# Mamba-2 scan of a decoder trunk without a chunk state, and with a group's sum of squares moved into the next group's insertion

## The reference, cut to what matters

```python
def step(state, inp):                    # L = 128, two chunks
    cum = jnp.cumsum(dtc * a, axis=1)
    decay = jnp.exp(jnp.where(causal, cum[:, :, None] - cum[:, None], -jnp.inf))
    w = jnp.einsum('bign,bjgn->bijg', cc, bc)[..., None] * decay * dtc[:, None]
    y = jnp.einsum('bijgh,bjghp->bighp', w, xc)
    y = y + jnp.einsum('bign,bghpn->bighp', cc, state) * jnp.exp(cum)[..., None]
    wts = jnp.exp(last[:, None] - cum) * dtc
    state = state * ... + jnp.einsum('bjgh,bjghp,bjgn->bghpn', wts, xc, bc)
# then: y + d_skip*x, times silu(z), RMS norm over each group's 512 channels, norm weight, w_out
```

## Time and profile before

| | us |
|---|---|
| median of 3 runs | 2580.13 (2579.45 to 2582.21) |
| the profiled execution | 2579.37 |
| its span | 2577.7 |
| PE busy | 2571.5 (100% of the span), granted clock full in all 40 slices |
| DVE busy | 1791.5 (70%) |
| ACT busy | 1419.8 (55%) |
| POOL busy | 220.4 (9%) |
| chain of work that ended last | PE 95%, DVE 3%, ACT 1% |

### The profile page before, as it was taken

How to read it: one execution, slowest core, us unless ns; L and a number is a source line. 1 busy time by engine, 2 the same in 40 slices (tenths; PEclk the granted TensorE clock), 3 DMA queues, 4 the chain that set the end, 5 groups by cost and what they waited for, 6 DMA issues and landing times.

```text
span 2577.7 us, 46139 instructions
## 1 busy us (share of the span) xinstructions
PE 2571.5 (100%) x15247; PEld 2255.1 (87%) x15247; DVE 1791.5 (70%) x2592; ACT 1419.8 (55%) x2190; POOL 220.4 (9%) x197
## 2 busy tenths in 40 slices
PE   9999999999999999999999999999999999999999
PEld 8888888888888888888888888888888888888888
DVE  8777777775677777776555686777777777775454
ACT  6776766754455555554444465665555555554333
POOL 0211122212100000000111000102200000000000
PEclk9999999999999999999999999999999999999999
DMA  6655555556555555556666576324555555556665
GB/s 213 234 193 192 195 196 195 196 179 188 188 188 190 189 186 191 190 191 183 191 190 190 193 235 198 121 98 137 183 191 189 187 189 191 190 187 187 189 190 169
DMA packets 139483, 481.59 MB, mean 187 GB/s; under 512 B 17329, under 2 KB 19441, under 8 KB 138384
## 3 DMA queue, kind: packets, MB, share of 16 engines
q1 hardware_dynamic: 136448, 467.20, 56.7%
q0 software_dynamic: 2368, 12.68, 1.4%
q10 hardware_dynamic: 592, 0.71, 0.1%
HBM read 478.28 MB, written 2.16 MB: 186 GB/s over the span
## 4 chain that ended last, share of the span: by engine, by line
PE 95%; DVE 3%; ACT 1%; issue 0%; DMA 0%; ACTq 0%; DVEq 0%
PE ps L844 49%; PE ps L843 26%; PE pq L844 6%; PE po L844 4%; PE pq L843 3%; PE po L843 2%; DVE w_lo L1268 1%; PE po L1151 1%; PE pq L1137 0%; PE ps L975 0%; PE ps L977 0%; PE ps L976 0%; PE ps L958 0%; PE pq L861 0%; PE po L965 0%
## 5 line engine op out<-in xcount | busy, mean ns | idle before, releaser
L1268 DVE TENSOR_TENSOR w_lo<-raw,w_hi 128x1024 fp32r<-128x1024 f32 (+1 forms) x896 | 1094.5, 1224 | 617.7 <-ACT w_hi L441 616.5
L441 ACT ACTIVATE w_hi<-raw 128x1024 fp32r<-128x1024 f32 (+1 forms) x896 | 933.5, 1043 | 808.1 <-PE ps L844 702.9
L844 PE MATMUL ps<-xn,w_hi 128*128 128x512 f32 x3904 | 1359.2, 392 | 0.0
L843 PE MATMUL ps<-xn,w_lo 128*128 128x256 f32 x3904 | 1098.3, 281 | 0.3 <-DVE gpad L1277 0.2
L844 PEld LDWEIGHTS ps<-xn,w_hi 128*128 128x128 f32 x3904 | 730.5, 187 | 159.6
L843 PEld LDWEIGHTS ps<-xn,w_lo 128*128 128x128 f32 x3904 | 737.8, 189 | 4.1 <-issue 1.5
L844 PE MATMUL ps<-hid,w_hi 128*128 128x512 f32 x1408 | 488.2, 391 | 0.0
L843 PE MATMUL ps<-hid,w_lo 128*128 128x256 f32 x1408 | 394.2, 280 | 0.0
L844 PEld LDWEIGHTS ps<-hid,w_hi 128*128 128x128 f32 x1408 | 263.3, 187 | 57.7
L843 PEld LDWEIGHTS ps<-hid,w_lo 128*128 128x128 f32 x1408 | 266.1, 189 | 0.0
L844 PE MATMUL pq<-xn,w_hi 128*128 128x512 f32 x528 | 185.3, 393 | 0.0
(11 more groups left out here) (300 smaller groups left out, 2461.4 us busy)
## 6 DMA issues: line engine op xcount, KB each, us to landing
raw<-w_gu SPq DMA_DIRECT2D x352, 512.0 KB, 3.9
raw<-w_ssm_in SPq DMA_DIRECT2D x158, 512.0 KB, 3.8
raw<-w_down SPq DMA_DIRECT2D x128, 448.0 KB, 3.4
raw<-w_nsa_in SPq DMA_DIRECT2D x82, 512.0 KB, 4.4
raw<-w_ssm_out SPq DMA_DIRECT2D x64, 512.0 KB, 4.4
raw<-w_down SPq DMA_DIRECT2D x64, 512.0 KB, 3.6
raw<-w_nsa_out SPq DMA_DIRECT2D x32, 512.0 KB, 4.4
wcum<-cum_scratch POOLq DMA_DIRECT2D x8, 1024.0 KB, 7.7
```

The lines of the kernel that those rows point to most:

```text
L441: act.activation(w_hi[:, slot, 0:n * P], raw[:, slot, 0:n * P], ACT.Copy).then_inc(unit_rounded, 1)
L843: pe.matmul(acc[:, n:2 * n], w_lo[:, slot, cols], x[:, kb, 0:n], start=(kb == 0), stop=False, skip_group_check=True)
L844: mm = pe.matmul(acc[:, 0:2 * n], w_hi[:, slot, cols], x[:, kb, 0:2 * n], start=False, stop=(kb == n_blocks - 1), skip_group_check=True)
L1268: TT(w_lo[:, slot, 0:n * P], raw[:, slot, 0:n * P], w_hi[:, slot, 0:n * P].bitcast(F32), ALU.subtract).then_inc(unit_split, 1)
```

## The change

The scan loses its state. `scan_turn` now has one product of B of the first chunk with C of both chunks (128x256) and one of B and C of the second chunk (128x128); the transpose of B, the state product and ACT's copy of the state are gone, `xw` stays as DVE made it, and POOL multiplies `cex` with the B0·C1 product from `sbt` (one third of it) where it took C from `bc`. `scan_y` is the same otherwise.

A group's sum of squares moves from behind unit 14 of its own scan pass to behind unit 0 of the next pass, ahead of the next group's `scan_turn`, and into another bank (`ps[7]`). What depends on it moves too: the root from step 14 to step 3 of the next pass, the scaling from 15 to 4, the rounding from 16 to 6, the rest from 17 to 7. The tables have a second number, 1 or 2, for how many groups back. POOL's skip term goes into a buffer of its own, `skip`, which lies where `y_ssm` lies; POOL no longer waits there for the previous group's `y_ready`.

```diff
@@ ACT
-            def scan_state(g):
-                act.wait_ge(state_done, g + 1)
-                act.activation(xw[:], ps[4][:], ACT.Copy).then_inc(state_ready, 1)
@@
-            SCAN_ACT = ((1, scan_sbt), (3, scan_ecum), (3, lambda g: scan_decay(g, 0)), (4, lambda g: scan_decay(g, 1)),
-                        (6, scan_state), (11, scan_square), (14, scan_std), (16, scan_round))
+            SCAN_ACT = ((1, 1, scan_sbt), (3, 2, scan_std), (3, 1, scan_ecum), (3, 1, lambda g: scan_decay(g, 0)),
+                        (4, 1, lambda g: scan_decay(g, 1)), (6, 2, scan_round), (11, 1, scan_square))
@@ ACT, last_scan_step
+                for at, back, stage in ((1, 1, scan_sbt), (2, 2, scan_std), (2, 1, scan_ecum), (2, 1, lambda g: scan_decay(g, 0)),
+                                        (2, 1, lambda g: scan_decay(g, 1)), (2, 1, lambda g: scan_decay(g, 2)), (4, 2, scan_round),
+                                        (6, 1, scan_square), (8, 1, scan_std), (9, 1, scan_round)):
@@ PE
-                pe.wait_ge(gstd_ready, g)
                 pe.wait_ge(yz_step, 2 * g)
...
-                    pe.matmul(ps[4][:, cut], bc[:, 0, cut], bc[:, 1, cut], start=True, stop=True)
-                pe.transpose(ps[4][:, 2 * L:3 * L], bc[:, 0, 0:L], ident[:]).then_inc(turned, 1)
-
-            def scan_state(g):
-                pe.wait_ge(xw_ready, g + 1)
-                pe.wait_ge(sbt_ready, g + 1)
-                pe.matmul(ps[4][:], sbt[:, 2 * L:3 * L], xw[:], start=True, stop=True).then_inc(state_done, 1)
+                pe.matmul(ps[4][:, 0:2 * L], bc[:, 0, 0:L], bc[:, 1], start=True, stop=True)
+                pe.matmul(ps[4][:, 2 * L:3 * L], bc[:, 0, L:T], bc[:, 1, L:T], start=True, stop=True).then_inc(turned, 1)
@@
             def scan_sumsq(g):
+                total = ps[4] if is_body(g, GROUPS - 1) else ps[7]
                 pe.wait_ge(sq_summed, g + 1)
-                pe.matmul(ps[4][:, 0:T], ones[:], xdt[:, 0, 0:T], start=True, stop=True).then_inc(gss_done, 1)
+                if not is_body(g, GROUPS - 1):
+                    pe.wait_ge(tile_out, ph["ssm"].tile0 + 9 + (g + 1) * ph["ssm"].per_body)
+                pe.matmul(total[:, 0:T], ones[:], xdt[:, 0, 0:T], start=True, stop=True).then_inc(gss_done, 1)
@@
-            SCAN_PE = ((0, scan_turn), (4, scan_state), (9, scan_y), (14, scan_sumsq))
+            SCAN_PE = ((0, 2, scan_sumsq), (0, 1, scan_turn), (9, 1, scan_y))
@@ PE, first body of ssm_out
-                for at, stage in ((0, scan_turn), (3, scan_state), (6, scan_y), (8, scan_sumsq)):
+                for at, back, stage in ((0, 2, scan_sumsq), (0, 1, scan_turn), (6, 1, scan_y), (8, 1, scan_sumsq)):
@@ DVE
-                    pair = yz[:, 2 * b:2 * b + 2].rearrange("p a t -> p (a t)")
-                    last = TT(pair, ps[2 + b][:], pair, ALU.add)
+                    last = TT(yz[:, 2 * b:2 * b + 2], ps[2 + b][:].rearrange("p (a t) -> p a t", a=2),
+                              skip[:, bass.ds(g * XT_G + 2 * b, 2), 0:T], ALU.add)
@@
-            SCAN_DVE = ((1, scan_xdt), (5, scan_w), (10, scan_yz), (15, scan_norm), (17, scan_rest))
+            SCAN_DVE = ((1, 1, scan_xdt), (4, 2, scan_norm), (5, 1, scan_w), (7, 2, scan_rest), (10, 1, scan_yz))
@@ DVE, last_scan_step
-                for at, stage in ((1, scan_xdt), (6, scan_yz), (8, scan_norm), (9, scan_rest)):
+                for at, back, stage in ((1, 1, scan_xdt), (2, 2, scan_norm), (5, 2, scan_rest), (6, 1, scan_yz), (8, 1, scan_norm),
+                                        (9, 1, scan_rest)):
@@ POOL
                 pool.wait_ge(conv_act, g * 6 + 6)
-                pool.wait_ge(y_ready, g)
...
-                pool.tensor_tensor(yz[:], xf[:], cst[:, bass.ds(g * XT_G + CONST["ssm_d"], XT_G)].unsqueeze(2).broadcast_to([P, XT_G, T]),
+                pool.tensor_tensor(skip[:, bass.ds(g * XT_G, XT_G), 0:T], xf[:], cst[:, bass.ds(g * XT_G + CONST["ssm_d"], XT_G)].unsqueeze(2).broadcast_to([P, XT_G, T]),
                                    ALU.mult).then_inc(xd_ready, 1)
...
-                pool.tensor_tensor(cex[:], cex[:], bc[:, 1, L:T].unsqueeze(1).broadcast_to([P, GH, L]), ALU.mult).then_inc(cex_ready, 1)
+                pool.wait_ge(sbt_ready, g + 1)
+                pool.tensor_tensor(cex[:], cex[:], sbt[:, L:2 * L].unsqueeze(1).broadcast_to([P, GH, L]), ALU.mult).then_inc(cex_ready, 1)
```

More of the change, by code:

```diff
@@ L201, in trunk @@
                 dt_odd = sb("dt_odd", [HEADS, T], F32, st2)
+            with ExitStack() as st3:
+                skip = sb("skip", [P, S_TILES, 2 * T], F32, st3)
             y_ssm = sb("y_ssm", [P, S_TILES, 2 * T], F32R, st)
@@ L513, in conv_silu @@
                     act.wait_ge(xd_ready, g)
-                else:
-                    act.wait_ge(cex_ready, g)
                 act.wait_ge(turned, g)
@@ L549, in scan_std @@
             def scan_std(g):
+                total = ps[4] if is_body(g, GROUPS - 1) else ps[7]
                 act.wait_ge(gss_done, g + 1)
-                act.activation(grs[:], ps[4][:, 0:T], ACT.Sqrt, scale=1.0 / (XT_G * P), bias=eps[:, 0:1]).then_inc(gstd_ready, 1)
+                act.activation(grs[:], total[:, 0:T], ACT.Sqrt, scale=1.0 / (XT_G * P), bias=eps[:, 0:1]).then_inc(gstd_ready, 1)
             def scan_round(g):
@@ L573, in ssm_body @@
                     if scan:
-                        for at, stage in SCAN_ACT:
-                            if at == v:
-                                stage(g - 1)
+                        for at, back, stage in SCAN_ACT:
+                            if at == v and (back == 1 or not is_body(g, 1)):
+                                stage(g - back)
                     else:
@@ L980, in scan_sumsq @@
             def scan_sumsq(g):
+                total = ps[4] if is_body(g, GROUPS - 1) else ps[7]
                 pe.wait_ge(sq_summed, g + 1)
-                pe.matmul(ps[4][:, 0:T], ones[:], xdt[:, 0, 0:T], start=True, stop=True).then_inc(gss_done, 1)
+                if not is_body(g, GROUPS - 1):
+                    pe.wait_ge(tile_out, ph["ssm"].tile0 + 9 + (g + 1) * ph["ssm"].per_body)
+                pe.matmul(total[:, 0:T], ones[:], xdt[:, 0, 0:T], start=True, stop=True).then_inc(gss_done, 1)
             p = ph["ssm"]
-            SCAN_PE = ((0, scan_turn), (4, scan_state), (9, scan_y), (14, scan_sumsq))
+            SCAN_PE = ((0, 2, scan_sumsq), (0, 1, scan_turn), (9, 1, scan_y))
             def ssm_body(g, scan=True):
                 for v in range(0 if scan else 4, p.body):
+                    if scan and v == 6 and not is_body(g, 1):
+                        pe.wait_ge(gstd_ready, g - 1)
                     gemm_unit(p, g, v, xn)
                     if scan:
-                        for at, stage in SCAN_PE:
-                            if at == v:
-                                stage(g - 1)
+                        for at, back, stage in SCAN_PE:
+                            if at == v and (back == 1 or not is_body(g, 1)):
+                                stage(g - back)
                     elif v == 15:
@@ L1395, in scan_w @@
                 for c in range(2):
-                    last = TT(wcum[:, :, c], wcum[:, :, c], sbt[:, c * L:(c + 1) * L].unsqueeze(1).broadcast_to([P, GH, L]), ALU.mult)
+                    last = TT(wcum[:, :, c], wcum[:, :, c], sbt[:, 2 * c * L:(2 * c + 1) * L].unsqueeze(1).broadcast_to([P, GH, L]), ALU.mult)
                 last.then_inc(w_ready, 1)
@@ L1436, in ssm_body @@
                     if scan:
-                        for at, stage in SCAN_DVE:
-                            if at == v:
-                                stage(g - 1)
+                        for at, back, stage in SCAN_DVE:
+                            if at == v and (back == 1 or not is_body(g, 1)):
+                                stage(g - back)
                     if taps:
```

19 lines of the change are left out of this document (10 added, 9 removed).

## The result

The changed kernel takes 2599.25 us (median of 4, 2599.09 to 2599.79) against 2579.92 us (median of 4, 2579.45 to 2582.21): 19.3 us more, a ratio of 1.0074 with a 95% interval of 1.0061 to 1.0086. It is slower, as forecast, inside the range of 2584 to 2602, and 5.2 us above the predicted 2594.1. Its profiled execution took 2599.3 us with a span of 2597.6, which is 19.9 above the span of before.

The account below looks back on a forecast made before the run. PE's work bounds the kernel as long as every unit is split before PE comes to it. Terms -6.2 - 1.7 + 16.8 + 3.2 + 1.8 = +13.9 us on 2579.4, plus 0.8 for the median: 2594.1; range 2584 to 2602.

Parts of the forecast that it names:

- the reserve of 2.7 us at unit 9: Pass 3: DVE's split of unit 9 ended 2.7 us before PE began the unit; anything beyond that makes PE wait.
- PE's own work: Turn, state and sum of squares on PE: each group 0.77 us cheaper, eight groups 6.2 us saved.
- the faster pairs: Pairs of PE products from turn to state step at 347 instead of 353 ns: 1.7 us saved in all.
- rival C: Pairs in the scan stay at the slow step through all passes: 7 us more, about 2602; chance 7%.
- The wait at unit 9: Moved root and scaling delay DVE's split, so PE waits 2.8 us in each of passes 2 to 7: +16.8.
- The rows' price for a table switch: ACT's table load ahead of the root costs 1.28 us with no drain; a 2.66 switch would add 8 us in all.
- What stands behind that wait: PE's pairs after the stop at unit 9: no term, so no cost was given for them.
- The skip product: POOL's multiplication, started earlier, runs beside the splits of units 18 and 19: 0.3 us a pass, +1.8 in all.
- Rival D: The skip product also stops PE at unit 18, a microsecond in each pass: 2599; chance 10%.
- The last group: PE waits 1.4 us before y and 1.8 before the sum of squares: +3.2 together, ends 1.5 to 4.
- Rivals A and B: Unit 9: A, split comes in time, 2572.2, chance 9%; B, wait about 1.3 a pass, 2581, chance 7%.
- the saving of 0.02 a group for the joining: Sum of squares placed directly ahead of the turn has no switch of its own: 0.02 us less a group.

## Why the prediction was right, step by step

- **What bounds the kernel, and the reserve of 2.7 us at unit 9: right.** The wait stands at the unit, in the passes and behind the instructions that the prediction names.
- **PE's own work and the faster pairs, -7.9: right.** Pass 1, which has no moved group, is 1.4 us shorter (its last pair starts at 137.63, not at 139.01; 1.3 forecast). A pass with all waits gone takes 60.7 us in the kernels with the sum of squares at 15, 1.0 under the 61.69 of before; 0.97 a group was forecast. The new turn left the pairs fast in every pass, so rival C is out (one stretch of 88 pairs was slow, behind y in pass 2: 0.6 us). The reason given, that the old turn ended in a transpose, is not shown: in the kernel with the state put back the same old turn stands directly behind the sum of squares, and the pairs behind it step by 347 ns in pass 2 (141.44 to 151.84, 30 steps). The term came out by a reason that stays open.
- **The wait at unit 9, 6 x 2.8 = 16.8: right.** The longest is 2.8 at the weight loads. By the distance of PE's weight loads at the six stops, less one step, they are five of 2.8 and one of 2.2, 16.1 in all. PE came at 225.2 on the clock of before (225.1 forecast), the split ended at 227.7 (228.0). The rows' price for a table switch, 1.28 us and nothing beside it, held: the root began 1.29 after its load.
- **What stands behind that wait: wrong, and the one large miss.** The prediction let PE go on after each stop as before. In fact the clock was at 1.2 GHz for the first five to seven pairs of unit 9, 1.2 to 1.6 us a pass; from the starts of the pairs it is 8.0 us in all, and the experiment that fills the wait gives 7.6. The sum priced a microsecond of waiting at a microsecond and no more; no term of it, and no rival, held this. The trace of before shows PE idle nowhere in the scan, so it had no row for it. With this term the sum would be 13.9 + 8.0 = 21.9.
- **The skip product, +1.8: wrong.** It ran beside the splits of units 18 and 19 as said (at 188.88 in pass 2, two splits in 4.56 us), but the split of unit 18 still ended 2.2 us or more before PE came, and PE did not stop: 0. Rival D is out. Without the join the same edit even gains 3.5 us. I had priced only whom the product meets at its new place, not whom it leaves in peace at its old one. This miss hid a part of the other: 21.9 - 1.8 = 20.1, against 19.9 by the spans. That the total lies within the range is in part luck: the range reached up to 2602 for rivals C and D, and neither came.
- **The last group, +3.2: right.** 1.4 before y and 1.8 before the sum of squares, read as 1.7 and 1.8 at the weight loads and as 1.36 and 1.46 on PE; the chains are those of the text. Neither made the clock fall.
- **Rivals A and B** fall with the row of unit 9. But A was one table entry away: with the scaling at step 3 the moved root is still there and the kernel takes 2578.0 (not A's 2572.2, since the last group's waits and some tenths at each split remain). The prediction took DVE's place ahead of unit 9 for full; it was, but 3.5 us of idle time lay one split earlier, in the row that it quoted.

Without the joining, the removed state is worth 3.8 us, and 7.6 with the skip buffer. The joining itself gives PE nothing. From the pair ahead of it to the pair behind it, less one step, the joined insertion costs 1.96 us (137.63 to 139.94 in pass 2); apart, in the kernel with the sum of squares at 15, the two cost 1.53 and 0.43, the same 1.96. So the saving of 0.02 a group for the joining is not there either.

## What to carry to other kernels

A wait that takes the place of work has two prices on the matrix engine, the wait itself and the clock behind it; look for the second in windows of a few microseconds, since the page's slices hide it. Before an operation is moved, ask on each engine between which two waits it lands: the same 3.5 us of scaling ahead of one split left the passes at 61.2 us, within 0.5 of a pass without any wait, and behind that split stopped PE six times. Taking work from the bounding engine gives nothing where it then waits for the same late partner.

## What the runs showed of the hardware

- After a stop of PE of 2.47 us in the row, the granted clock was at 1.2 GHz for the first pairs. In pass 7 the stop was shorter, and the clock fell as well:

```profile
488.84 0.39 PE L841 MATMUL ps<-xn,w_lo 128*128 128x256 f32 x1 [1.91 <-DVE w_lo L1267]
...
489.45 0.41 PE L841 MATMUL ps<-xn,w_lo 128*128 128x256 f32 x1
...
490.09 0.41 PE L841 MATMUL ps<-xn,w_lo 128*128 128x256 f32 x1
```

  After stops of 1.63 and 1.62 (state put back), 1.46 and 1.36 (last group) and 0.96 (root as a copy) it stayed at 2.4. These are single stops in single traces; no run shows whether the length alone decides.
- The pairs have two steps, 347 and 353 ns, at the same full clock; the longest stretches are 463 pairs fast and 439 slow. Between 60 and 560 us of all twelve traces, an insertion that PE does not wait for left fast pairs fast, with three exceptions: the turn of the kernel before, an insertion at 63 us, ahead of the scan (slow behind it in five traces), and two of the six fillings of the wait. Behind slow pairs the products of y left them slow in 8 of 16 cases. Behind a stop, even one of 0.03 to 0.05 us, the step comes out either way. Where it turned slow with no insertion and no stop of 0.1 us or more (up to 760 us), this was at the first pair of a unit, and in all such cases but one DVE had ended the operand that PE needed for it only 0.1 to 0.3 us before. In the traced executions the step behind unit 12 of the output projection goes with the heap. What decides it stays open.
